# Stick-breaking layer: the product of weights and values of one pass is issued in the middle of the next pass, ahead of its scores

## The reference, cut to what matters

```
z = h @ w_in                                  # (272, 8192)
q, k, v, gate = split(z, 4)
for each block of 128 queries, each head:
    z  = (q * 128**-0.5) @ k.T                # scores of the keys before the query
    sp = softplus(z) where visible, else 0
    tail = suffix sums of sp over the keys
    w  = exp(z - tail) where visible, else 0
    o  = w @ v
y = (o * silu(gate)) @ w_out
h = layer_norm(alpha * h + y)
```

## Time and profile before

| | |
|---|---|
| median of 3 runs | 905.19 us (904.98 to 906.22) |
| profiled execution | 904.98 us, its span 903.1 us |
| PE busy | 894.1 us, 99% of the span |
| PEld busy | 862.2 us, 95% |
| DVE busy | 556.5 us, 62% |
| ACT busy | 428.2 us, 47% |
| DMA | 153.05 MB, 169 GB/s on the mean |

### The profile page before, as it was taken

One profiled execution on the slowest core, in us unless ns is written; L12 is line 12 of the kernel. 1 busy time (PEld: TensorE's weight loads), 2 busy tenths in 40 slices (PEclk: granted clock), 3 DMA queues, 4 the chain that ended last, 5 costly groups with the idle time before them and its releaser, 6 DMA issues.

```text
span 903.1 us, 17875 instructions
## 1 busy us (share of the span) xinstructions
PE 894.1 (99%) x7182; PEld 862.2 (95%) x7182; DVE 556.5 (62%) x744; ACT 428.2 (47%) x683; POOL 62.8 (7%) x85
## 2 busy tenths in 40 slices
PE   9999999999999999999999999999999999999997
PEld 9999999999999999899999999999999999988886
DVE  6578667667765767785646464555646355545546
ACT  6556455645655344375454343535444444435421
POOL 1322133113100000000000000000000000000000
PEclk9999999999999999999999999999999999999999
DMA  9774465455442555515453444444354534454622
GB/s 350 234 234 163 157 213 146 145 168 177 152 150 110 187 187 187 187 63 213 145 187 139 176 149 165 160 144 181 139 186 139 186 141 167 157 215 159 233 93 94
DMA packets 25256, 153.05 MB, mean 169 GB/s; under 512 B 3411, under 2 KB 3939, under 8 KB 8709
## 3 DMA queue, kind: packets, MB, share of 16 engines
q1 hardware_dynamic: 21600, 142.19, 43.9%
q0 software_dynamic: 2896, 7.70, 4.2%
q10 hardware_dynamic: 724, 2.66, 0.8%
HBM read 150.36 MB, written 2.18 MB: 169 GB/s over the span
## 4 chain that ended last, share of the span: by engine, by line
PE 94%; DMA 2%; DVE 2%; ACT 1%; SPq 1%; issue 0%; DVEq 0%
PE bank L333 70%; PE bank L703 10%; PE bank L448 2%; PE bank L488 2%; DMA work<-chunks 1%; DMA raw<-chunks 1%; PE bank L648 1%; PE bank L647 1%; PE bank L650 1%; PE bank L615 1%; PE bank L574 1%; PE bank L588 1%; DVE w_lo L1061 1%; PE bank L463 0%; PE bank L616 0%
## 5 line engine op out<-in xcount | busy, mean ns | idle before, releaser
L333 PE MATMUL bank<-x_hi,w_hi 128*128 128x272 f32 (+1 forms) x1472 | 425.6, 289 | 0.0
L333 PE MATMUL bank<-x_hi,w_lo 128*128 128x272 f32 (+1 forms) x1472 | 421.4, 286 | 0.0
L333 PE MATMUL bank<-x_lo,w_hi 128*128 128x272 f32 (+1 forms) x1472 | 421.3, 286 | 0.0
L1061 DVE TENSOR_TENSOR w_lo<-raw,w_hi 128x2048 fp32r<-128x2048 f32 x126 | 290.8, 2312 | 207.5 <-ACT w_hi L782 174.3
L782 ACT ACTIVATE w_hi<-raw 128x2048 fp32r<-128x2048 f32 x114 | 217.8, 1912 | 156.7 <-PE bank L333 108.2
L333 PEld LDWEIGHTS bank<-x_hi,w_hi 128*128 128x128 f32 x1472 | 277.4, 188 | 1.3 <-issue 0.4
L333 PEld LDWEIGHTS bank<-x_hi,w_lo 128*128 128x128 f32 x1472 | 277.3, 188 | 0.0
L333 PEld LDWEIGHTS bank<-x_lo,w_hi 128*128 128x128 f32 x1472 | 277.1, 188 | 0.0
L333 PE MATMUL bank<-og_hi,w_hi 128*128 128x272 f32 x240 | 70.1, 292 | 0.0
L333 PE MATMUL bank<-og_hi,w_lo 128*128 128x272 f32 x240 | 69.4, 289 | 0.0
L333 PE MATMUL bank<-og_lo,w_hi 128*128 128x272 f32 x240 | 69.1, 288 | 0.0
(11 more groups left out here) (243 smaller groups left out, 1019.0 us busy)
## 6 DMA issues: line engine op xcount, KB each, us to landing
raw<-chunks SPq DMA_DIRECT2D x128, 1024.0 KB, 4.8
work<-bias_table POOLq DMA_DIRECT2D x8, 512.0 KB, 5.6
work<-chunks SPq DMA_DIRECT2D x4, 512.0 KB, 12.4
work<-bias_table POOLq DMA_DIRECT2D x8, 256.0 KB, 6.6
work<-ln_rows ACTq DMA_DIRECT2D x1, 2048.0 KB, 7.3
out<-work SPq DMA_DIRECT2D x8, 256.0 KB, 2.4
h<-xT SPq DMA_DIRECT2D x2, 544.0 KB, 9.5
raw<-chunks SPq DMA_DIRECT2D x4, 256.0 KB, 5.1
```

What stands on the lines that cost most here:

```text
L333: last = mm(o, l, r, start=(kt == 0 and n == 0), stop=(kt == KT - 1 and n == 2))
L1061: V.tensor_tensor(lo_part, raw[:, half, :, :], hi_part.bitcast(f32), ALU.subtract) \
```

## The change

`attend_b(i)` is no longer issued behind the projections of pass i, but in pass i + 1 between the halves of P+2, directly ahead of `scores_b(i + 1)`. For the last pass it is issued behind the loop. The gated output follows it on DVE and ACT (`gated_b`, `gated_lo_b`, `gated_hi_b`). On DVE the multiply of u stands ahead of the limiting of the scores of u and the subtraction behind it. On ACT both roundings stand ahead of Abs. In passes 1 to 7 DVE's `split_lo(P + 4, 0)` is moved from behind the limiting of the scores to behind the copy of the values of u = 0, where pass 0 already has it.

```diff
@@ tensor engine, body_b
-                project(P + 2, x_hi, x_lo, ALL, between=lambda: scores_b(i),
+
+                def meet():
+                    if not isinstance(i, int):
+                        attend_b(i - 1)
+                    scores_b(i)
+
+                project(P + 2, x_hi, x_lo, ALL, between=meet,
                         banks=v_acc_0 if isinstance(i, int) else None, layer_b=True)
...
                 project(P + 3, x_hi, x_lo, SEQ_COLS, between=mid, layer_b=True)
-                attend_b(i)
 
             body_b(0)
             with pe.Fori(1, B_ITERS) as i:
                 body_b(i)
+            attend_b(B_ITERS - 1)
@@ scalar engine
+            def gated_hi_b(i):
+                for u in range(2):
+                    act.wait_ge(o_read, O_A + 2 * i + u + 1)
+                    A(og_hi[:, 2 * i + u, 0:SEQ], b["og"], ACT.Copy).then_inc(og_hi_ready, 1)
...
                 act.wait_ge(pv_done, PV_A + 2 * i)
+                if not isinstance(i, int):
+                    gated_hi_b(i - 1)
...
                 split_hi(P + 5, 1, True)
-                for u in range(2):
-                    act.wait_ge(o_read, O_A + 2 * i + u + 1)
-                    A(og_hi[:, 2 * i + u, 0:SEQ], b["og"], ACT.Copy).then_inc(og_hi_ready, 1)
@@ vector engine
+            def gated_b(i, u):
+                dve.wait_ge(pv_done, PV_A + 2 * i + u + 1)
+                dve.wait_ge(tile_free[u], P_B + 4 * i + 4)
+                dve.wait_ge(og_lo_ready, O_A + 2 * i + u)
+                V.tensor_tensor(b["og"], o_b[:, u, :], b["gate"][:, u, :], ALU.mult).then_inc(o_read, 1)
+
+            def gated_lo_b(i, u):
+                dve.wait_ge(o_read, O_A + 2 * i + u + 1)
+                dve.wait_ge(og_hi_ready, O_A + 2 * i + u + 1)
+                V.tensor_tensor(og_lo[:, 2 * i + u, 0:SEQ], b["og"], og_hi[:, 2 * i + u, 0:SEQ].bitcast(f32),
+                                ALU.subtract).then_inc(og_lo_ready, 1)
...
-                for u in range(2):
+                before = not isinstance(i, int)
+                for u in range(2):
+                    if before:
+                        gated_b(i - 1, u)
                     dve.wait_ge(z_ready, 2 * i + u + 1)
                     z = both(z_bank[u][:, 0:128], B_K1)
...
-                if not isinstance(i, int):
-                    split_lo(P + 4, 0, True)
...
+                    if before:
+                        gated_lo_b(i - 1, u)
...
-                    if u == 0 and isinstance(i, int):
+                    if u == 0:
                         split_lo(P + 4, 0, True)
```

More of the change, by code:

```diff
@@ L1025, in _ @@
                 body_b(i)
+            gated_hi_b(B_ITERS - 1)
             act.wait_ge(og_lo_ready, O_A + KT)
@@ L1347, in body_b @@
                      .then_inc(z_capped, 1)
-                z = z_bank[1][:, B_K2:B_K2 + B_L]
-                V.tensor_tensor(z, z, cap[:, 256:256 + B_L], ALU.min).then_inc(z_capped, 1)
-                if not isinstance(i, int):
-                    split_lo(P + 4, 0, True)
+                    if u:
+                        z = z_bank[1][:, B_K2:B_K2 + B_L]
+                        V.tensor_tensor(z, z, cap[:, 256:256 + B_L], ALU.min).then_inc(z_capped, 1)
+                    if before:
+                        gated_lo_b(i - 1, u)
                 parts = [(z_bank[u][:, 0:c.stop - c.start], b["w"][:, c], b["sp"][:, c]) for u, c in enumerate(B_HEADS)]
@@ L1394, in _ @@
                 body_b(i)
+            for u in range(2):
+                gated_b(B_ITERS - 1, u)
+                gated_lo_b(B_ITERS - 1, u)
             dve.wait_ge(r_ready, 8)
```

## The result

The changed kernel takes 912.86 us (median of 6 runs, 912.62 to 913.26) against 905.35 us before (6 runs): a ratio of 1.0083, 95% interval 1.0072 to 1.0094. It is slower by 7.5 us. The forecast was 910.6 us, with a range to 914.8.

The account below looks back on a forecast made before the run. PE's own instruction stream was taken to bound the kernel. The gate's and value copy's waits, 0.72 + 6 x 0.50 + 7 x 0.26 = 5.54 us, on the median of 905.19 gave 910.6 us, range 907.2 to 914.8.

Parts of the forecast that it names:

- PE's stream bounds the kernel, the move can win nothing: Passes 1 to 7: PE has no idle time, no instruction is removed, so the saving on PE is taken as 0.
- The crossing between the two fp32 blocks: On PE, between `attend_b` and the scores: saving taken as 0, at most 0.11 us a pass, 0.8 us in all.
- The gate's wait: P+4's first load waits for bank 0 until the gate's last DVE step: 0.72 us once, then 0.50 a pass.
- The value copy's wait: P+3 waits for bank 0 until the first value copy, late behind the gated output: 0.26 us a pass, bounds 0 to 0.45.
- The chain of gated outputs: On DVE and ACT ahead of Abs: 2.72 us from the first multiply to the end of the second rounding.
- The split, the transfer and the gate are level: Late split of (P+4, 0) delays the next transfer; DVE's following split ends about when the gate is due, adding 0.02 us.
- Gate alone: Rival: value copy stays hidden, only the gate's wait counts, 0.11 us a pass saved between fp32 blocks: 908.0 us, chance 0.17.
- Faster: Rival on PE: no bank wait binds and each merged fp32 pair saves its whole step: 904.4 us, chance 0.03.
- no more than 1.8 us: Rival: PE's waits are partly absorbed, less than 0.26 us a pass is left: 906.2 us, chance 0.08.
- The granted clock: Rival: idle time between matmul groups lowers PE's clock to 1.2 of 2.4 GHz, costing 40 us: 945 us, chance 0.02.
- the rule of a load pulled ahead: At PE's 14 bank waits: pulling weight loads ahead would shorten each by some 0.12 us, 1.7 in all; prediction rejected it.

Follow-up runs that it names:

- experiment 5: Changed kernel with the gate of every pass (P+3) accumulated in the two free banks 4 and 7: 904.90 us against 905.09 for the kernel before, ratio 1.0001.
- experiment 2: Changed kernel with the queries of passes 1 to 7 accumulated in the two free banks: 908.99 us, ratio 1.0041 to the kernel before.
- Experiment 6: Kernel before, with only PE's `attend_b` moved between the halves of the next pass's first projection; DVE and ACT as before: 909.03 us, ratio 1.0041.
- experiment 3: Changed kernel with the values of all passes accumulated in the two free banks: 911.38 us, ratio 1.0066 to the kernel before.
- experiment 4: Changed kernel with values in the two free banks and the split of (P+4, 0) ahead of the softplus again: 908.96 us, ratio 1.0043 to the kernel before.
- experiment 1: Changed kernel with `attend_b` back at the end of its own pass on PE, DVE and ACT as changed: 917.23 us, ratio 1.0132 to the kernel before.

## Why the prediction was right or wrong

- **PE's stream bounds the kernel, the move can win nothing.** Right. Without bank waits the new order is worth 0.0 us (experiment 5). The crossing between the two fp32 blocks: their first loads are 1.59 us apart in the changed kernel (623.50 and 625.09), the block cost 1.58 before, so 0 was the value and not 0.11.
- **The gate's wait: foreseen 0.72 + 6 x 0.50 = 3.7 us, found 0.82 + 6 x 0.55 = 4.1 in the gaps, 3.9 by experiment 2.** The mechanism holds. The small excess is the wake: I took 0.05 us from the end of the gate to the load, as in pass 0; in the hardware loop it is 647.31 - 647.18 = 0.13. Experiment 6 reproduces it from the kernel before with one edit.
- **The value copy's wait: foreseen 0.26 us a pass, found 0.56.** This is the term that was mis-sized: 7 x 0.30 = 2.1 us, as good as all that the forecast lacked, and it lies above the 0.45 that I had set as its upper bound. The chain of gated outputs itself was read well: from the first multiply to the end of the second rounding 2.74 us against 2.72. What was wrong were three joints, two of which make the copy 2.45 us later relative to the scores' old place and not 2.2. The rows of the changed kernel (L978 is the rounding of the gated output, L1007 Abs, and L1013 in the rows of the result is Ln):

```profile
623.50 0.32 PEld L615 LDWEIGHTS bank<-work 128*128 128x128 f32 x2
...
624.98 0.30 PE L618 MATMUL bank<-work 128*128 128x32 f32 x2
...
625.52 0.42 DVE L1350 TENSOR_TENSOR work<-bank,work 128x256 f32<-128x256 f32 x1 [3.16 <-PE bank L618]
...
627.84 0.42 ACT L978 ACTIVATE og_hi<-work 128x256 f32 x1 [1.36 <-DVE work L1350]
...
628.16 0.91 ACT L1007 ACTIVATE work<-bank 128x400 f32<-128x400 f32 x2
```

First, DVE starts the first multiply 625.52 - (624.98 + 0.30) = 0.24 us behind the block's last matmul, where I took 0.13. Second, I let DVE win 0.15 us at the softplus, on the guess that the weight split held it there. It is not won: from the start of Abs to that of the softplus are 630.48 - 628.16 = 2.32 us now, and were 625.68 - 623.34 = 2.34 behind the split, so the Ln and not the split set its start before as well. Third, the wake behind the copy is 0.11 us and not 0.05. Together they are 0.32, to a rounding the whole difference of 0.30.

- **The split, the transfer and the gate are level.** Right in size and, as experiments 3 and 4 show, the one place where the waits depend on each other. As foreseen, ACT's split of (P+5, 0) now waits for the transfer. From the end of DVE's split of (P+4, 0) to ACT's start were 4.83 to 5.08 us in the seven passes, against the 5.06 of pass 0. In the pass with the longest, 579.81 + 2.28 = 582.09 to 587.17, the chain that ended last reaches the gate by way of the transfer:

```profile
582.27 4.88 DMA raw<-chunks
...
587.17 1.92 ACT w_hi L788
...
589.12 2.29 DVE w_lo L1072
591.41 0.28 DVE work L1401
```

In the next pass it comes from PE, and the gate's gap is 0.55 us in both. In experiment 3 the gate pays for it as soon as PE comes earlier.

- **The rivals.** "Gate alone" is what experiments 2, 4 and 6 look like from either side, near 909. "Faster" and "no more than 1.8 us" fell. The granted clock stayed at 1.00 in the stretch with its 14 gaps of 0.55 to 0.82 us, and also with the seven of 1.76 us in experiment 1. The weight load did wait behind the bank's semaphore, as in pass 0; the rule of a load pulled ahead, which the prediction cites from the Trainium skill, "TensorE: Matmul & The Clock Gate", section "Step-by-step: what each phase is for", did not show across a wait.
- **A slip in the sum.** 905.19 + 5.54 is 910.7 and not 910.6 us. It changes nothing.

## What to carry to other kernels

Before a block is moved on the engine that sets the time, ask what else it was doing where it stands: 1.58 us of other work between two users of a bank was what let a four-step chain of 3 us free it in time. Then ask what the moved work's followers on the other engines are put in front of, there and in their queues, and how late their release will be. If banks are free, giving the slow reader its own is the test of such a theory and the cure in one, and it shows at once whether the new order was worth anything.

## What the runs showed that I had not expected

The view of waits gave 4.6 us for the two waits where the gaps between weight loads sum to 8.0 us and the measured time grew by 7.5: the matmuls' modelled ends cover some 0.24 us of a gap, (8.0 - 4.6) / 14. And a load behind a semaphore started 0.05 us after the release in pass 0, which is written out, but 0.11 to 0.13 us after it in the hardware loop.
